# RWKV chunks of a two-layer encoder: where the transposed triangle comes from

## The reference, cut to what matters

```
def step(s, xs):
    r_t, w_t, k_t, v_t, a_t, b_t = xs
    sa = einsum('bhvk,bhk->bhv', s, a_t)
    s = s * w_t + sa[..., None] * b_t + v_t[..., None] * k_t
    return s, einsum('bhvk,bhk->bhv', s, r_t)
```

## Time and profile before

| | us |
|---|---|
| median of 3 runs | 4039.81 (4038.9 to 4042.9) |
| profiled execution | 4039.59 |
| its span | 4037.8 |
| PE busy | 3603.0 |
| VectorE busy | 1857.6 |
| ScalarE busy | 1028.2 |

### The profile page before, as it was taken

The page is one execution under the profiler, slowest core; times in us unless marked ns, Lnnn a source line. Parts: engine busy times, 40 slices in busy tenths (PEclk is TensorE's granted clock), DMA queues, the critical chain, the costliest instruction groups (busy, mean ns, idle before and its releaser), DMA issues. The chain is left out here.

```text
span 4037.8 us, 74421 instructions
## 1 busy us (share of the span) xinstructions
PE 3603.0 (89%) x31490; PEld 3420.7 (85%) x31490; DVE 1857.6 (46%) x2270; ACT 1028.2 (25%) x1395; POOL 1195.3 (30%) x574
## 2 busy tenths in 40 slices
PE   8998887979999999898997876777688999999988
PEld 7997786969999999798996445777678999999978
DVE  1653554255454454744412225545445554544563
ACT  2454333032111111221013334222322111111131
POOL 3333432333333333343332000000043333333342
PEclk9998998989999999999998988998899999999999
DMA  3111001001111111112211016121200111111101
GB/s 123 57 50 50 1 0 72 31 21 45 44 42 42 47 42 42 43 36 98 92 66 46 1 61 197 35 42 27 103 31 32 42 46 42 42 42 47 53 22 68
DMA packets 99768, 203.89 MB, mean 50 GB/s; under 512 B 57824, under 2 KB 59104, under 8 KB 98464
## 3 DMA queue, kind: packets, MB, share of 16 engines
q1 hardware_dynamic: 92528, 160.26, 12.3%
q10 hardware_dynamic: 7088, 41.33, 2.6%
HBM read 164.34 MB, written 37.23 MB: 50 GB/s over the span
## 5 line engine op out<-in xcount | busy, mean ns | idle before, releaser
L712 PE MATMUL PS<-XH,WHI 128*128 128x274 f32 x5248 | 1531.7, 292 | 93.8 <-DVE XL L2052 31.7
L712 PE MATMUL PS<-XL,WHI 128*128 128x274 f32 x5248 | 1529.6, 291 | 0.0
L712 PE MATMUL PS<-XH,WLO 128*128 128x274 f32 x5248 | 1526.9, 291 | 0.0
L801 POOL TENSOR_TENSOR WHI<-RAW,EPS 128x1024 fp32r<-128x1024 f32 x218 | 417.4, 1915 | 2470.4 <-PE PS L712 2428.9
L712 PEld LDWEIGHTS PS<-XH,WHI 128*128 128x128 f32 x5248 | 999.6, 190 | 100.0 <-issue 48.5
L712 PEld LDWEIGHTS PS<-XL,WHI 128*128 128x128 f32 x5248 | 1001.6, 191 | 0.0
L712 PEld LDWEIGHTS PS<-XH,WLO 128*128 128x128 f32 x5248 | 1000.6, 191 | 0.0
L804 POOL TENSOR_TENSOR WLO<-RAW,WHI 128x1024 fp32r<-128x1024 f32 x218 | 569.5, 2612 | 17.1
L712 PE MATMUL PS<-HH,WHI 128*128 128x274 f32 x1408 | 410.9, 292 | 15.3 <-DVE HL L2077 13.1
L712 PE MATMUL PS<-HH,WLO 128*128 128x274 f32 x1408 | 408.6, 290 | 0.0
L712 PE MATMUL PS<-HL,WHI 128*128 128x274 f32 x1408 | 407.6, 290 | 0.0
(11 more groups left out here) (399 smaller groups left out, 4648.1 us busy)
## 6 DMA issues: line engine op xcount, KB each, us to landing
RAW<-in_units SPq DMA_DIRECT2D x218, 512.0 KB, 3.2
prepared_rows<-PREP SPq DMA_DIRECT2D x8, 1096.0 KB, 5.6
CIN<-prepared_rows SPq DMA_DIRECT2D x17, 512.0 KB, 5.3
c_rows<-DX ACTq DMA_DIRECT2D x14, 548.0 KB, 2.8
RKV<-c_rows SPq DMA_DIRECT2D x4, 1644.0 KB, 9.9
X<-in_x SPq DMA_DIRECT2D x8, 548.0 KB, 9.0
XR<-in_x ACTq DMA_DIRECT2D x1, 4384.0 KB, 18.4
x_rows<-Y ACTq DMA_DIRECT2D x1, 4384.0 KB, 12.9
```

What stands on the lines that cost most here:

```text
L712: last = nc.tensor.matmul(PS[:, 4 * slot + b, 0:width], wt[:, ring, w], r[:, k, b * width:(b + 1) * width], start=n == 0, stop=n == 3 * nk ...
L801: nc.gpsimd.tensor_tensor(WHI[:, s, :], RAW[:, s, :], ZERO.to_broadcast([128, 1024]), ALU.add)\
```

## The change

PE issues the gram a second time with its operands exchanged (B_S and ARI), right behind l, into the other half of the same bank: that is L transposed ("lt"). VectorE masks it with a new constant FIRST_TURNED, the transposed mask of level 0, into TT_S and subtracts that from the identity. The product with the identity goes, and with it the step prep3. tt0 and lm1 move into prep2, ahead of rb, ak and rk; VectorE waits for lt instead of l. w1 waits for rk and for ScalarE's KT, since it writes over the bank that these read. FIRST and SECOND have eight names each, and w3 is now the last of the first half.

```
--- before.py
+++ after.py
@@ -384,6 +384,7 @@
             "B_S", "K_S", "LM_S", "W_S", "TA_S", "TT_S", "AK_S", "BT_S", "KT_S", "VT_S", "PI_S", "RB_S", "RK_S", "X_S", "U_S")]
         PX = both("PX", 4, 65)
         PAIR_LEVEL = room("PAIR_LEVEL", [128, 6, 64])
+        FIRST_TURNED = room("FIRST_TURNED", [128, 64])
 
         TAIL = SLAB // 32 * 32
         CO = at("CO", [128, 4, NT], TAIL - 4 * TILE)
@@ -557,8 +558,8 @@
         G_FIRST = ["decays", "diffs", "grams", "blocks", "w1", "t1", "w2", "t2", "w3"]
         G_SECOND = ["t3", "w4", "t4", "w5", "t5", "w6", "t6", "carry1", "carry2"]
         C_LEVELS = range(1, 6)
-        FIRST = ["prep0", "prep1", "prep2", "prep3", "w1", "t1", "w2", "t2"]
-        SECOND = ["w3", "t3", "w4", "t4", "w5", "t5", "carry1", "carry2", "carry3"]
+        FIRST = ["prep0", "prep1", "prep2", "w1", "t1", "w2", "t2", "w3"]
+        SECOND = ["t3", "w4", "t4", "w5", "t5", "carry1", "carry2", "carry3"]
 
         class ChunkStages:
 
@@ -581,11 +582,11 @@
                             *[x + str(l) for l in range(1, 7) for x in ("tt", "ta")][:-1], "r", "s")
         G_ACT = ChunkStages("staged", "exps", "ko", "vb", *["w%d" % l for l in range(1, 7)], "v_new", "out")
         G_POOL = ChunkStages("upper", "m1", "q_in", *["m%d" % l for l in range(2, 7)])
-        C_PE = ChunkStages("vt", "l", "kg", "bg", "mt",
+        C_PE = ChunkStages("vt", "l", "lt", "kg", "bg",
                            *[x + str(l) for l in C_LEVELS for x in (("lw", "tt", "ta") if l < 5 else ("lw", "tt"))],
                            "x", "u", "o", "m")
         C_ACT = ChunkStages("px", "pi", "vt", "bt", "kt", *["w%d" % l for l in C_LEVELS], "x", "u", "o")
-        C_DVE = ChunkStages("scan", "as", "bs", "kb", "rs", "lm0", "ta0", "rb", "ak", "rk", "tt0", "lm1",
+        C_DVE = ChunkStages("scan", "as", "bs", "kb", "rs", "lm0", "lt0", "ta0", "tt0", "lm1", "rb", "ak", "rk",
                             *[x for l in C_LEVELS for x in (["lm%d" % (l + 1), "tt%d" % l, "ta%d" % l] if l < 5 else ["tt5"])],
                             "m0", "m")
 
@@ -1259,6 +1260,7 @@
                     pe.wait_ge(c_dve[p], C_DVE.at(j, "bs"))
                     tiled()
                     c_heads(stacked(b), ARI[p][:, :, 0:64], B_S[p]).then_inc(s, 1)
+                    c_heads(stacked(b, 1), B_S[p], ARI[p][:, :, 0:64]).then_inc(s, 1)
                     pe.wait_ge(c_dve[p], C_DVE.at(j, "rs"))
                     tiled()
                     for m in range(4):
@@ -1269,13 +1271,10 @@
                     pe.wait_ge(c_act[p], C_ACT.at(j, "vt"))
                     tiled()
                     c_heads(per_head(b + 3), B_S[p], ARI[p][:, :, 64:192]).then_inc(s, 1)
-                elif name == "prep3":
-                    pe.wait_ge(c_act[p], C_ACT.at(j, "kt"))
-                    pe.wait_ge(c_dve[p], C_DVE.at(j, "rk"))
-                    tiled()
-                    c_heads(stacked(b + 1), LM_S[p], PAIR_ID).then_inc(s, 1)
                 elif name[0] == "w":
-                    pe.wait_ge(c_dve[p], C_DVE.at(j, "tt%d" % (level - 1) if level > 1 else "lm1"))
+                    pe.wait_ge(c_dve[p], C_DVE.at(j, "tt%d" % (level - 1) if level > 1 else "rk"))
+                    if level == 1:
+                        pe.wait_ge(c_act[p], C_ACT.at(j, "kt"))
                     tiled()
                     c_heads(stacked(b + 1), LM_S[p], TT_S[p]).then_inc(s, 1)
                 elif name[0] == "t":
@@ -2282,10 +2281,16 @@
                     nc.vector.tensor_tensor(ARI[p][:, :, 64:128], r, PX[p][:, :, 1:65], ALU.mult).then_inc(s, 1)
                 elif name == "prep2":
 
-                    dve.wait_ge(c_pe[p], C_PE.at(j, "l"))
+                    dve.wait_ge(c_pe[p], C_PE.at(j, "lt"))
                     level_blocks(0, p).then_inc(s, 1)
+                    nc.vector.tensor_tensor(TT_S[p][:, :, :], stacked(4 * p, 1), pairs_of(FIRST_TURNED[:, :]), ALU.mult)\
+                        .then_inc(s, 1)
                     dve.wait_ge(s, C_DVE.at(j, "lm0"))
                     nc.vector.tensor_tensor(TA_S[p][:, :, :], pairs_of(PAIR_ID), LM_S[p][:, :, :], ALU.subtract).then_inc(s, 1)
+                    dve.wait_ge(s, C_DVE.at(j, "lt0"))
+                    nc.vector.tensor_tensor(TT_S[p][:, :, :], pairs_of(PAIR_ID), TT_S[p][:, :, :], ALU.subtract).then_inc(s, 1)
+                    dve.wait_ge(s, C_DVE.at(j, "ta0"))
+                    level_blocks(1, p).then_inc(s, 1)
                     dve.wait_ge(c_pe[p], C_PE.at(j, "bg"))
                     upper, strict = small("pair_upper", 64), small("pair_strict", 64)
                     nc.vector.scalar_tensor_tensor(RB_S[p][:, :, :], per_head(4 * p + 3)[:, :, 0:64], -1.0, pairs_of(upper),
@@ -2295,11 +2300,6 @@
                             out[p][:, :, :].rearrange("p (b m) n -> p b m n", b=2),
                             k_group(p).rearrange("p b (m n) -> p b m n", m=2)[:, :, :, first:first + 64],
                             mask.unsqueeze(1).unsqueeze(1).to_broadcast([128, 2, 2, 64]), ALU.mult).then_inc(s, 1)
-                elif name == "prep3":
-                    dve.wait_ge(c_pe[p], C_PE.at(j, "mt"))
-                    nc.vector.tensor_tensor(TT_S[p][:, :, :], pairs_of(PAIR_ID), stacked(4 * p + 1), ALU.subtract).then_inc(s, 1)
-                    dve.wait_ge(s, C_DVE.at(j, "ta0"))
-                    level_blocks(1, p).then_inc(s, 1)
                 elif name[0] == "w":
                     if level < 5:
                         dve.wait_ge(c_pe[p], C_PE.at(j, "lw%d" % level))
@@ -2350,6 +2350,9 @@
             for h in range(2):
                 nc.vector.tensor_copy(PAIR_LEVEL[half(h), :, :],
                                       small("level", 6 * 128).rearrange("p (l c) -> p l c", l=6)[half(h), :, half(h)])
+            step(nc.vector.memset(FIRST_TURNED[:, :], 0.0))
+            nc.vector.tensor_copy(FIRST_TURNED[:, :].rearrange("p (t o) -> p t o", o=2)[:, :, 1],
+                                  PAIR_ID.rearrange("p (t o) -> p t o", o=2)[:, :, 0])
             step(nc.vector.memset(RUN[:, :], 1.0))
             nc.vector.memset(RUN[:, :].rearrange("p (c t) -> p c t", t=64)[:, :, 0:1], 0.0)
             for p in range(2):
```

More of the change, by code:

```diff
@@ L2297, in c_step @@
                             mask.unsqueeze(1).unsqueeze(1).to_broadcast([128, 2, 2, 64]), ALU.mult).then_inc(s, 1)
[L2298 to L2302, removed]
                 elif name[0] == "w":
```

## The result

| | before | changed |
|---|---|---|
| median, us | 4041.36 (4 runs) | 4018.30 (4 runs) |
| ratio, 95% interval | | 0.9940 (0.9923 to 0.9957) |
| profiled execution's span | 4037.8 | 4017.8 |

A forecast was written before the change was run, and what follows sets the result against it. It took one chain over three engines, with PE waiting in it, to bound the chunk step. Plain steps +10, edges +4 and start-up −0.7 gave +13.3 us: 4053 us, 8-in-10 range 4037 to 4068.

The forecast's parts named there:

- The plain steps: Ten joint chunk steps without a loop edge: t3' to w1 grows by 1.0 us each, +10 us (1 to 14).
- rival (3): Ordinary chunk steps: PE's wait before t4' drops the clock, twelve falls, +22 us, about 4075 us; chance 0.13.
- Across an edge: Six loop back edges: PE's standing stays and covers w3's copy, clock may return later; +0.7 each, +4 us (−1 to +11).
- rival (2): Back edges: second standing of 2.00 us disappears, 6 x −2 = −12, about 4028 us; chance 0.11.
- Start-up: Lone first half at half clock: mt's 1.62 us of chain goes, lt adds 0.88, −0.7 us.

The follow-up runs named there:

- seven-piece runs: Changed products with the halves paired as before, TensorE's loop body cut to 1789 or 1791 instructions and shifted to fit seven pieces: 3985.29 and 3982.36 us.
- the spread filler: Changed kernel plus 225 semaphore increments spread over places where TensorE waits anyway, putting its loop body at the earlier kernel's place in a piece: 4055.39 us.
- the old pairing and the loop written out: Changed products and masks with the halves paired as in the kernel before, TensorE's loop of seven passes written out: 3986.54 us.
- the changed kernel written out: Changed kernel with TensorE's loop of seven passes written out, the other engines keeping theirs: 4006.10 us.

## Why the prediction was wrong

**The plain steps: right, at 0.85 for 1.0 us.** t3' to w1 takes 9.75 us (2533.97 to 2543.72) where 9.92 was worked out, PE stands 1.42 before t4' (1.64 forecast) and 1.18 before w1 (1.36). The copy follows PI by 0.30, not 0.33. The clock stays at 1.00 in these steps: rival (3) didn't happen.

**The step that failed: "Across an edge", in its first sentence.** The prediction took "PE's standing of about 5.3 us" as given for all six edges, and only asked what it would cover. It fell away at four of them, because there PE's program was not loaded again: whether an edge stands goes with how far the loop's body runs into an eighth piece (six edges at 237 instructions, two at 8), which the change moved by the way. The edges gave 35 us in all, against a cost of 4 that the prediction added for edges. This was the result of rival (2), which had 0.11, and not by its reason: that reason was that the jump would land on products whose inputs are ready, and the kernel before with 31 increments lands on the same w3' as ever and loses the standing as well, at three of six edges. Its own argument against, that what was missing were the instructions, was the right reading of "issue"; the prediction then wrongly went on that they would be missing after the change too. The page "Runtime: NRT & Kernel Launch" of the Trainium skill (Instruction fetch mechanics), which it cited for that, also gives PE 2048 instructions in blocks of 256. The seven-piece runs agree as far as they go: 1789 and 1791 instructions stay, 74 packets; no run here has a body near 2048 that stays. It says too that only a target inside a window of two blocks is spared; in the seven-piece runs the jump goes back seven blocks and nothing is loaded, so the measurement decides against that part. Counting the body was possible before the result: it is 1802 instructions, and the compiled programs of the two kernels have it 31 apart. That the eighth piece decides is known only from the runs.

**In numbers.** From the second scan to the last the stage fell from 318.25 to 295.71 us, by 22.5; the rest of the gain is in the first step (below). The plain-step loss of 0.85 for each of the 15 steps in that stretch is 12.8, so the edges gave 35.3 us. Before, a step across an edge took 26.0 us on average from mt to mt, 8.2 more than a plain one: 5.2 of standing and, behind it, the half clock. Four such edges are 33 us, and the two that still stand cost less than before, 4.7 of standing. Where all six stand (the spread filler), a pass of two steps takes 2.1 us more than before, 0.85 of it the plain step, so a step across an edge cost 1.2 more, where the forecast had taken 0.7.

**The forecast as a statement on the order of work was right.** With the body at the old place the changed kernel runs in 4055.4 us, inside the range and 2 us from the 4053. That it is so near is partly luck: up to 2 us of it are the filler's, the ten plain steps cost 8.5 and not 10, the six across an edge 7 and not 4.

**Start-up.** −0.7 was forecast; from the first to the second scan it is 18.63 before and 16.41 after. With the old pairing and the loop written out it is 14.81, with the changed kernel written out 18.19. The granted clock from 2489 to 2495 is 0.51 before and 1.00 in the changed kernel, and in the changed kernel written out it is 0.50 again from 2488 to 2491. So a part of the 2.2 seems to go with how long the low clock lasts there. The share of the change in it wasn't separated.

## What to carry to other kernels

When an edit adds, removes or moves instructions ahead of a long loop, count the loop's body in instructions and where it begins, and read the line of instruction loads and the "issue" waits at the back edge first: a body a little over seven pieces gained or lost 21 to 37 us here for the same work. Compare two orders of work with the body at the same place in its piece, or written out, before saying which is better. And when a step drops out of one of two interleaved lists, write down the new pairing for every engine: the product that was replaced was worth 1.0 us per step, the new neighbours cost 1.8.

## What the runs showed of the hardware that was not expected

- A body of 1789 or 1791 instructions that fits seven pieces is loaded once (74 packets in all); one of 1798 to 1802 with 8 to 68 instructions in an eighth piece is loaded again in every second or third pass (101 or 92 packets), and with 232 or more in every pass (128 or 129). A pass that loads takes nine packets.
- In the passes that load and the ones that don't, the order of work is the same, so a timeline of one pass doesn't tell the cost of the next: edges at 0.21 and 4.62 us follow each other in one run.
- 225 semaphore increments took 35 us on PE, 0.15 us each, though the profile shows 51 ns for one.
- Straight code has small waits too: 17 us of "issue" in 260 us of the stage written out, ordinary spacings among them, and none in the run where nothing is loaded.
